# Delta rule with its triangular blocks inverted at 16x16 on 128 partitions instead of 32x32 on 64, its decay rows by a selector, and a window attention with fused row minima

## What is computed

```python
# delta rule, per head and chunk: a unit lower triangular system
diff = G[..., :, None] - G[..., None, :]          # G: cumulated log gates
t_mat = eye + b[:, None] * exp(diff) * (k @ k.T)  # strictly lower part
w_mat = triangular_solve(t_mat, b * exp(G) * k)
u_v   = triangular_solve(t_mat, b * v)
def step(S, ...):                                 # sequential over chunks
    u = uv_c - w_c @ S
    o = qd_c @ S + intra_c @ u
    S = exp(gl_c) * S + kt_c.T @ u

# attention: latent queries, keys within 128 tokens, 256 context keys, a sink
p = softmax(concat([s_loc + mask, s_ctx, s_sink]))
o = p[local] @ v + p[context] @ v_ctx
```

## Time and profile before

| | us |
|---|---|
| median of 3 runs | 3681.94 |
| lowest, highest | 3679.02, 3684.13 |
| the profiled execution, its own time | 3679.53 |
| its span in the trace | 3677.7 |
| TensorE busy | 3455.9 (94%) |
| VectorE busy | 1802.4 (49%) |
| ScalarE busy | 1175.1 (32%) |
| GpSimd busy | 693.2 (19%) |

### The profile page before, as it was taken

The page is one execution under the profiler, slowest core; times in us unless marked ns, Lnnn a source line. Parts: engine busy times, 40 slices in busy tenths (PEclk is TensorE's granted clock), DMA queues, the critical chain, the costliest instruction groups (busy, mean ns, idle before and its releaser), DMA issues. The chain is left out here.

```text
span 3677.7 us, 49398 instructions
## 1 busy us (share of the span) xinstructions
PE 3455.9 (94%) x19822; PEld 2656.2 (72%) x19822; DVE 1802.4 (49%) x3343; ACT 1175.1 (32%) x2057; POOL 693.2 (19%) x528
## 2 busy tenths in 40 slices
PE   7999999999999999999976767988999999999998
PEld 6767778878888888875545656556887478888886
DVE  4277971233785554345577884678211243223222
ACT  3276751222211111234434453158111131112110
POOL 1190000110101111010020110048001213333333
PEclk9999999999999999999988887999999999999999
DMA  3101111121233322113012124000123011111111
GB/s 136 38 2 41 41 49 44 58 96 53 92 98 101 100 92 81 63 51 126 1 27 44 35 48 140 18 1 2 43 75 102 4 58 58 46 46 46 58 46 46
DMA packets 266352, 211.84 MB, mean 58 GB/s; under 512 B 65680, under 2 KB 231184, under 8 KB 265744
## 3 DMA queue, kind: packets, MB, share of 16 engines
q1 hardware_dynamic: 264368, 201.61, 17.7%
q10 hardware_dynamic: 1760, 7.08, 0.9%
HBM read 185.33 MB, written 21.50 MB: 56 GB/s over the span
## 5 line engine op out<-in xcount | busy, mean ns | idle before, releaser
L95 PE MATMUL ps<-halves 128*128 128x512 f32 x10408 | 2407.3, 392 | 18.4 <-DVE halves L1546 6.6
L95 PEld LDWEIGHTS ps<-halves 128*128 128x128 f32 x10408 | 1954.7, 188 | 441.3 <-issue 28.3
L95 PE MATMUL ps<-arena 128*128 128x512 f32 (+1 forms) x880 | 367.9, 572 | 8.0 <-issue 3.4
L1525 POOL TENSOR_TENSOR tmps<-tmps 128x512 f32<-128x512 f32 x128 | 143.9, 1124 | 979.6 <-ACT tmps L1493 979.6
L1546 DVE TENSOR_TENSOR halves<-tmps,halves 128x512 fp32r<-128x512 f32 x128 | 89.0, 698 | 432.2 <-ACT halves L1501 432.2
L1429 ACT ACTIVATE halves<-raws 128x2048 fp32r<-128x2048 f32 x62 | 118.4, 1909 | 554.8 <-PE ps L95 532.4
L95 PEld LDWEIGHTS ps<-arena 128*128 128x128 f32 x880 | 165.9, 193 | 168.4 <-issue 157.3
L1532 POOL TENSOR_TENSOR arena<-arena 128x512 f32<-128x512 f32 x128 | 164.7, 1294 | 191.4 <-DVE arena L1573 191.4
L1493 ACT ACTIVATE tmps<-ps 128x512 f32<-128x512 f32 x128 | 76.6, 598 | 363.7 <-PE ps L95 353.7
L1573 DVE TENSOR_TENSOR arena<-ps,arena 128x512 f32<-128x512 f32 x128 | 87.7, 690 | 194.9 <-PE ps L95 188.4
L1369 DVE SCALAR_TENSOR_TENSOR arena<-arena,sc 128x128 f32<-128x128 f32 x448 | 163.3, 365 | 15.9
(11 more groups left out here) (303 smaller groups left out, 3235.7 us busy)
## 6 DMA issues: line engine op xcount, KB each, us to landing
raws<-in_w_ff SPq DMA_DIRECT2D x31, 1024.0 KB, 6.7
raws<-in_w_mlp SPq DMA_DIRECT2D x31, 1024.0 KB, 5.2
mixw<-in_w_in SPq DMA_DIRECT2D x56, 512.0 KB, 3.8
arena<-in_w_ada SPq DMA_DIRECT2D x48, 512.0 KB, 3.9
arena<-in_w_in SPq DMA_DIRECT2D x5, 2048.0 KB, 12.0
arena<-in_x SPq DMA_DIRECT2D x8, 1024.0 KB, 8.4
h_stash<-arena SPq DMA_DIRECT2D x1, 5120.0 KB, 30.5
inverses<-arena ACTq DMA_DIRECT2D x20, 256.0 KB, 2.9
```

The costliest lines, as they stand in the source:

```text
L95: ins = e.matmul(out_ap, l, r, start=i == 0, stop=i == n - 1)
L1525: e.tensor_tensor(tt, tt, tt, ALU.mult).then_inc(*f_sq.tick())
```

## The change

1. **Blocks of 16.** The diagonal blocks that go through DRAM are 16x16: 128 blocks of 256 elements on 128 partitions. `vector_inverse` takes k = 1 to 14 (`PART = 7` cuts it in two). Reading the blocks out takes 16 DMAs a chunk, and the inverses come back by 8 DMAs (`Z0`) and 16 DMAs (`ZT`).
2. **A new join.** `tensor_join16_a`, `vector_join16`, `tensor_join16_b` and `scalar_join16_b` join pairs of 16 to blocks of 32 (`YC`) by products. 8 DMAs within the core's memory place these in `YT` (`sync_inverses_placed`).
3. **Decay rows.** `gpsimd_gates` is gone. The cumulated gates are made once for all chunks (`vector_decay_parts`, `scalar_decay_parts`, `sync_decay_parts`, 4 DMAs), split in two float32r parts; each decay row product is then a selector column times these rows, in float32r.
4. **Orders.** SP brings all inverses of n before it reads out the blocks of n+1. ScalarE writes out the inverse before `step_b`, `tensor_keys(n+2, 0)` stands ahead of `tensor_join_c`, the decay rows shift by one join. `DECAYS` is 6 instead of 9.
5. **Fused attention.** A combined VectorE instruction adds the mask, negates, writes and takes the row minimum, for all four score tiles. The maxima of line 2890 and both plain copies go. VectorE scales the second head, GpSimd the first.

```diff
-        PARTS = 18, 24
+        PART = 7
@@ vector_inverse
-                e.tensor_tensor(T3, bc(W3[:, k:k + 1, k + 1:32], [64, k, 31 - k]),
-                                bc(W3[:, 0:k, k:k + 1], [64, k, 31 - k]), ALU.mult)
+                e.tensor_tensor(T3, bc(W3[:, k:k + 1, k + 1:16], [P, k, 15 - k]),
+                                bc(W3[:, 0:k, k:k + 1], [P, k, 15 - k]), ALU.mult)
@@ sync_inverses
+                e.wait_ge(*bk.full(("ja", n - 1)))
+            for dd, q in [(dd, q) for dd in range(2) for q in range(4)]:
+                b = 2 * q + dd
+                e.dma_start(Z0[dd][blk16(b), :, blk16(dd)], ...)
+            if n:
+                e.wait_ge(*bk.full(("jy", n - 1)))
+            for dd in range(2):
+                for b in range(8):
+                    e.dma_start(ZT[dd][blk16(b), :, blk16(b % 2)], ...)
@@ sync_delta
-            for n in range(1, 10):
-                if n < 9:
-                    sync_blocks(e, n + 1)
-                sync_inverses(e, n)
-                if n < 9:
-                    sync_blocks_in(e, n + 1)
-                sync_inverses_turned(e, n)
+            for n in range(10):
+                sync_inverses(e, n)
+                if n < 9:
+                    sync_blocks(e, n + 1)
+                    sync_blocks_in(e, n + 1)
+                sync_inverses_placed(e, n)
@@ tensor_decay_rows
-            chain(e, o[:, :], [(ones, IT[n % 3][dd][:, s * 4:s * 4 + 4, :]),
+            chain(e, o[:, :], [(bc(E2[:, c:c + 1], [P, 128]), GR[:, :, s, :]),
@@ vector_watt
-                        e.tensor_tensor(z[:, s, 0:nl], bk.tile(("wl", i, s))[:, 0:nl], wn[:, m0:m0 + nl], ALU.add)
+                        e.tensor_tensor_reduce(out=z[:, s, 0:nl], in0=bk.tile(("wl", i, s))[:, 0:nl],
+                                               in1=wn[:, m0:m0 + nl], scale=-1.0, scalar=nsk[...],
+                                               op0=ALU.add, op1=ALU.min, accum_out=c[:, 4 + s:5 + s])
-                        e.tensor_reduce(c[:, s:s + 1], z[:, s, 0:nl + 256], AX.X, ALU.max, negate=True)
+                    e.tensor_scalar(p, p, c[:, 7:8], None, ALU.mult).then_inc(*w_rc.tick())
```

More of the change, by code:

```diff
@@ L2144, in scalar_decay_rows @@
             e.wait_ge(*e_sv.at(2))
+            if n < 3:
+                e.wait_ge(*bk.full(("ci", 11, 1024) if n else ("ci", 7, 512)))
+            else:
+                e.wait_ge(*(bk.full(("so", n - 3, dd)) if latent(n - 3, dd) else bk.clear(("kk", n - 3, dd, 1))))
             e.wait_ge(*bk.full(key))
```

332 lines of the change are left out of this document (202 added, 130 removed).

## The result

| | before | changed |
|---|---|---|
| median, us | 3683.03 | 3738.32 |
| lowest, highest | 3679.02, 3687.69 | 3736.32, 3744.11 |
| runs | 4 | 4 |
| the profiled execution, its own time | 3679.53 | 3739.82 |

The changed kernel is slower: ratio 1.0152, 95% interval 1.0135 to 1.0170, some 55 us. The prediction was 3734, slower with a chance of 0.87.

A forecast was written before the change was run, and what follows sets the result against it. TensorE was taken to bound most of the kernel, VectorE the delta rule and attention; after the change SP's DMA starts and the joins set the delta rule. 3679.5 + 64 (delta rule) - 10 (attention) = 3733.5 us, range 3690 to 3785.

The forecast's parts named there:

- The bound that moves: Delta rule: VectorE sheds 16 us a turn, but 19 us of SP and 17 of joins in series replace its 25.
- The series of starts: SP, from S (start of a turn's first Z0 DMA): 39 starts at 0.49 us, 19.1; next blocks requested at +21.4, before +2.3.
- From the blocks to the next S: Delta rule, copy of the landed blocks (+24.0) through joins and ScalarE's writing of the inverse to the next Z0 start (+45.8).
- the 2.9 us for join_b's bank: TensorE's join_b waits for step_o's bank, freed by VectorE's sum at +31.3 against +28.4, in each turn.
- The turn: One delta rule turn takes 46 us, 43 for turns 1 and 2, 37.3 before; bounds 41.5 and 51; turns 1 to 8 +63.
- The start: Delta rule up to S(1): S(0) comes 5 us earlier and turn 0 takes 43 instead of 49.1, together -11 us.
- The last turn: Turn 9 of the delta rule, from S to the last solve: 32 us instead of 20.4, +12.
- The attention: Fused attention: VectorE saves 0.5 us a pair, 16 in all; taken as -10 us, with 0 as the other end.
- The sign that I named, VectorE idle: Attention after the change: 4.1 us a pair with VectorE idle.
- VectorE was the bound, so its relief shows: Rival, delta rule: SP's series is short, so the kernel is faster; 3643 us with transfers near 0.25 us; chance 0.08.
- Slower still: Rival: SP stalls within its series and TensorE runs the joins at the low clock; 52 us a turn, 3790; chance 0.15.
- The rule that I weighed, some 50 ns of dispatch: Page's figure for starting a DMA: 40 in a row delay the request some 2 us; turn 29 us, kernel about 3572.

The follow-up runs named there:

- experiment 2: The changed kernel with the old attention put back, so the changed delta rule alone: 3759.58 us, ratio 1.0213 to the kernel before.
- experiment 3: The kernel before with 16 spare DMAs on SP between its inverses and its request for blocks: 3769.33 us, ratio 1.0242.
- experiment 4: The changed kernel with the 16 DMAs that read out the blocks started by GpSimd instead of SP: 3664.47 us, ratio 0.9955.
- experiment 7: The changed kernel with each of the 14 multiplies of a turn's inverse on VectorE issued twice: 3751.63 us, ratio 1.0189.
- experiment 10: As experiment 4, with TensorE's step_a ahead of the new join's second half and VectorE's direction-0 sum and step_a ahead of the inverse: 3671.63 us.

## Why the prediction was right

**The bound that moves.** Right. VectorE's relief of 100 us in eight turns bought nothing, because it waits for blocks that SP asks for 24 us into the turn.

**The series of starts (19.1 us to the last start, request at +21.4).** The price of 0.49 a start was right and a little high for one start (the row of 2298.19: 3.62 us for 8 without a stall, so (3.62 - 0.43) / 7 = 0.46), but single starts in a series take 1.1 to 1.9 us, three or four times in the 40 starts of a turn. I had seen one such case in the earlier trace rows (1.93 for four) and put it into the high end only. The measured request is at +24.0 in the turn shown, 2.6 us later. In the eight turns the copy of the blocks starts at +26.2 on average, where the sum had +24.0.

**From the blocks to the next S (21.8).** Measured 21.4 in the turn shown (2136.54 to 2157.98), but 20.1 on average over the eight turns (18.0 to 21.6). The term that was mis-sized is the 2.9 us for join_b's bank: the wait is 0.5 to 1.3 us in five turns, 5.2 in all. VectorE's sum came about when I had it (6.8 us behind the start of the copy of the blocks, 7.3 in the sum), but TensorE was not ready for join_b as early as in the old trace. Between join_a and join_b it now runs step_o of direction 1 (1.98 us) and the decay rows (1.22), at a granted clock of 0.50. A term that I put at nothing cost something: join_c waited for the placed blocks for 6.2 us in all, in turns 1, 2 and 8, where they landed at about +35 and not +31.

Over the eight turns the way to the blocks was 18 us longer than the sum had it, and the way from there 8 us shorter. The two errors cancel in part, which is luck.

**The turn.** Predicted 46 with 43 for turns 1 and 2; measured 46.3, and 45.8 and 46.1 for those two. In these two the later blocks are 4.9 us of the error. Without step_o join_b does follow join_a after 2.2 us there instead of 5.3, but join_c then waited 2.1 and 1.3 us for the placed blocks. The two turns are 5.9 of the 8 us by which turns 1 to 8 were short (+71.5 against +63).

**The start (-11).** A step that failed: measured S(1) is 5.0 us earlier, not 11. Turn 0 took 44.8 us instead of 43, and S(0) came 0.7 us earlier than before, not 5. ScalarE's wait of 4.25 us for the first inverse did go: its second write was started at 1879.18 and landed 1.7 us later. But SP's first Z0 waits by the code for GpSimd's clearing of buffers as well (`s_zero`), for three memsets where the kernel before waited for one, and the last of them ended at 1883.15:

```profile
1876.91 3.52 POOL L2731 MEMSET arena<- 128x4096 f32 x1 [95.68 <-PE ps L95]
1880.37 2.78 POOL L2732 MEMSET arena<- 128x2560 f32 x1
...
1883.22 3.64 SPq L2317 DMA_DIRECT2D arena<-inverses  x8
```

The prediction has no term for that wait, which holds SP 2.3 us longer than the inverse does. GpSimd began the clearing when TensorE was through with a tile of the short convolution, 3.9 us later than in the kernel before (1876.91, and 1872.97 for GpSimd's first work there). Why TensorE came late there I have not followed.

**The last turn (+12).** Measured 2331.62 - 2298.19 = 33.4 against 20.4: +13. The delta rule's sum is -5.0 + 71.5 + 13.1 = +79.6 at its last solve, where +64 was forecast; experiment 2 (the delta rule alone) gives +77.5 for the time.

**The attention (-10).** Predicted 0.5 us a pair, 16 in all, cut to 10, with 0 as the other end. Measured -20.5 alone, and -19.3 from the last solve to the end of the trace (1406.4 us against 1425.6). The combined instructions cost 479 ns for 256 elements, where I had 410, and 610 for 384, their reads 82, and the 640-element scaling 553 (0.55). VectorE's sum was right: in the two windows it is busy for 15.7 us less (126.9 and 111.2). What was mis-sized is the comparison: I took VectorE's sum as the whole effect. Between 2430 and 2571 TensorE was idle for 141.0 - 119.7 = 21.3 us in the kernel before, of which 10.2 for GpSimd's scaling, 5.7 for ScalarE's copy of the fourth score tile and 4.4 for VectorE's mask:

```profile
PE ps L2826 <- POOL arena L2949: 10.2, 16, 1.4
...
PE ps L2826 <- ACT arena L2916: 5.7, 10, 0.6
```

With the change that copy is gone and TensorE is idle for 2.4 us in 118, so its own 3.7 us a pair is the floor. The sign that I named, VectorE idle, did not come: it is busy for 94% of the stretch.

Two misses, 15 too little for the delta rule and 10 too little for the attention's gain, leave +55 against +54. That the totals agree so well is luck; the terms don't.

**Rivals.** "VectorE was the bound, so its relief shows" falls with experiments 3, 4 and 7. "Slower still" had its mechanism right (stalls and the low clock are both there) and its size wrong. The rule that I weighed, some 50 ns of dispatch (the Trainium skill, "DMA: Bandwidth & Descriptors", section "Anatomy of one DMA — SWDGE (gpsimd) path"), gives, as an estimate, a kernel near 3572. A start takes 528 ns on GpSimd's own queue and 431 on SP's, so the trace agrees on neither.

## What to carry to other kernels

Count the starts that stand in a queue ahead of the one that somebody waits for: here each costs 0.46 us and 0.56 with its share of stalls, for 8 KB and (experiment 3) for 32 KB, so a layout change that halves the bytes of the blocks and takes SP from 22 DMAs a turn to 50 can lose. When a step is made shorter, put the longest chain that doesn't contain it beside it before counting the gain. When DMAs must be many, split them over queues whose engines are idle then; GpSimd's gave back 74 of the 77 us that the delta rule lost, and with the inverses on two queues as well the same change takes 0.99 of the time of the kernel before.

## What the runs showed of the hardware that I had not expected

- A start on SP or ScalarE takes 431 or 452 ns at the median, but up to 2080 in a series; on GpSimd it takes 528 in 144 starts with a longest of 729. GpSimd is slower by one and steadier by the series.
- A DMA of 32 KB from the core's memory to itself costs SP 612 ns a start, where one of 8 KB from DRAM costs 431 and one of 32 KB, in the kernel before, 451.
- TensorE pauses for 0.4 to 2.8 us at fixed instructions, in programs with long rows of 32x32 products 11 ns apart: 13 us of a stretch of 270 in the changed kernel, 25 in experiment 10. Each pause ends 1.2 to 1.6 us after a 16 KB packet of instructions has landed.
- 32x32 products on one corner of the array take 43 ns a record, spread over four places 11 ns.
- VectorE's scaling of 128x1024 (line 1963) took 2.99 us once, beside GpSimd's memset of line 2731; the median of the line's 20 is 0.75.
